# Attention scores with their sign turned: the minimum of the negated scores taken as the bias of the exponentials

## The reference

```python
# first block: 8 heads of 64, causal, with a forget bias
scores = einsum('bqhd,bkhd->bhqk', q_i, k) * scale        # scale = 1/8
scores = scores + c_i[:, :, :, None] - c[:, :, None, :]   # c = cumsum(log_sigmoid(f))
probs = softmax(where(causal, scores, -inf))
out = einsum('bhqk,bkhd->bqhd', probs, v)
# second block, both layers: 4 heads of 64 over 256 memory rows
p = softmax(einsum('bshd,bmhd->bhsm', q, k) * scale); o = p @ v
# second block, second layer: 6 pairs of heads
s = where(allowed, q k^T - slope * |t - pos|, -inf); p = softmax(s)
attn = p[:, :, 0] - lam * p[:, :, 1];  o = attn @ v
```

## Time and profile before

| | us |
|---|---|
| median of three executions | 3593.1 |
| lowest of three executions | 3591.57 |
| the profiled execution | 3596.61 |
| its span in the trace | 3595.3 |
| mean granted TensorE clock over the span | 0.896 |

### The profile page before, as it was taken

The page is one execution under the profiler, slowest core; times in us unless marked ns, Lnnn a source line. Parts: engine busy times, 40 slices in busy tenths (PEclk is TensorE's granted clock), DMA queues, the critical chain, the costliest instruction groups (busy, mean ns, idle before and its releaser), DMA issues.

```text
span 3595.3 us, 49969 instructions
## 1 busy us (share of the span) xinstructions
PE 2998.4 (83%) x20746; PEld 2384.4 (66%) x20746; DVE 1708.5 (48%) x3078; ACT 1071.2 (30%) x1867; POOL 655.5 (18%) x525
## 2 busy tenths in 40 slices
PE   5997857879999999699999677777768899877787
PEld 3775646668888888477886466666556678644466
DVE  2424544454444444665541576775435222466454
ACT  5213454531111111643112122122435111344533
POOL 1112123321111110342110122221014121000013
PEclk8998878989999999899999699998579999888769
DMA  2201003101111111122121000002022112100122
GB/s 71 57 24 59 24 6 117 53 30 53 48 46 54 47 47 47 35 82 71 53 65 63 1 3 3 3 3 90 1 70 70 59 55 68 56 1 1 53 68 73
DMA packets 197458, 164.55 MB, mean 46 GB/s; under 512 B 5312, under 2 KB 173930, under 8 KB 196082
## 3 DMA queue, kind: packets, MB, share of 16 engines
q1 hardware_dynamic: 197234, 161.36, 14.4%
HBM read 138.24 MB, written 23.10 MB: 45 GB/s over the span
## 4 chain that ended last, share of the span: by engine, by line
PE 66%; DVE 15%; ACT 9%; issue 6%; POOL 2%; DMA 2%; DVEq 0%; SPq 0%; ACTq 0%; POOLq 0%
PE ps L659 13%; PE ps L660 13%; PE ps L661 13%; PE ps L1896 5%; PE ps L1597 4%; PE ps L1564 3%; PE ps L1589 2%; ACT sb L1612 2%; PE ps L1302 1%; PE ps L1303 1%; PE ps L1304 1%; DVE r L634 1%; PE ps L700 1%; ACT r L629 1%; PE ps L702 1%
## 5 line engine op out<-in xcount | busy, mean ns | idle before, releaser
L659 PE MATMUL ps<-r,r 128*128 128x512 f32 (+1 forms) x2304 | 930.5, 404 | 131.2 <-DVE r L634 115.3
L660 PE MATMUL ps<-r,r 128*128 128x512 f32 (+1 forms) x2304 | 913.5, 396 | 0.0
L661 PE MATMUL ps<-r,r 128*128 128x512 f32 (+1 forms) x2304 | 911.2, 395 | 0.0
L659 PEld LDWEIGHTS ps<-r,r 128*128 128x128 f32 x2304 | 446.0, 194 | 246.4 <-DVE r L634 115.0
L615 POOL TENSOR_TENSOR sb<-sb 128x1024 f32<-128x1024 f32 x138 | 274.8, 1998 | 1297.4 <-DMA sb<-in_w_ffn_up 491.5
L660 PEld LDWEIGHTS ps<-r,r 128*128 128x128 f32 x2304 | 446.5, 194 | 95.6 <-issue 5.7
L661 PEld LDWEIGHTS ps<-r,r 128*128 128x128 f32 x2304 | 445.8, 193 | 94.2
L1896 PE MATMUL ps<-sb 64*64 64x64 f32 (+2 forms) x8832 | 302.9, 227 | 123.3 <-DVE sb L2146 29.3
L1896 PEld LDWEIGHTS ps<-sb 64*64 64x64 f32 (+1 forms) x8832 | 281.8, 136 | 152.4 <-issue 100.7
L634 DVE TENSOR_TENSOR r<-sb,r 128x1024 fp32r<-128x1024 f32 x198 | 260.4, 1322 | 231.6 <-ACT r L629 231.4
L629 ACT CAST r<-sb 128x1024 fp32r<-128x1024 f32 x198 | 204.9, 1043 | 350.3 <-POOL sb L615 350.1
(11 more groups left out here) (266 smaller groups left out, 3710.7 us busy)
## 6 DMA issues: line engine op xcount, KB each, us to landing
sb<-in_w_out SPq DMA_DIRECT2D x36, 512.0 KB, 4.1
sb<-in_a_w_in SPq DMA_DIRECT2D x29, 512.0 KB, 4.0
sb<-in_w_ffn_gate SPq DMA_DIRECT2D x22, 512.0 KB, 3.9
sb<-in_w_ffn_up SPq DMA_DIRECT2D x22, 512.0 KB, 3.9
sb<-in_w_ffn_down SPq DMA_DIRECT2D x22, 512.0 KB, 3.4
gates<-sb SPq DMA_DIRECT2D x36, 256.0 KB, 2.0
sb<-in_w_in SPq DMA_DIRECT2D x17, 512.0 KB, 4.0
sb<-in_x SPq DMA_DIRECT2D x16, 512.0 KB, 5.6
```

Of the source, the lines that this page charges most:

```text
L659: pe.matmul(self.out, w.hi[:, q, self.cols], hi, start=(q == 0), stop=False)
L660: pe.matmul(self.out, w.hi[:, q, self.cols], lo, start=False, stop=False)
L661: ins = pe.matmul(self.out, w.lo[:, q, self.cols], hi, start=False, stop=(q == w.nk - 1))
```

## The change

q is multiplied by -1/8 in place of 1/8 in all places where it is evicted, so PE delivers negated scores. The biases change their sign too: the scan in `Forget` gives c and not -c, the mask is +1e30, and the distances stay positive. The reduction takes the minimum, which is the negated maximum, and ACT computes exp(-(value) + minimum) by `scale=-1.0`. The 128x1 multiplication by -1 and DVE's wait ahead of it are gone, the event `maxed` with them: ACT waits for `biased`. In `Lambda.dve` the multiplication of the 128x1024 distances by -1 and the wait behind it are gone.

```diff
-            ("negc", [ATT_H, S]), ("xs", [P, KT, S]), ...
+            ("c", [ATT_H, S]), ("xs", [P, KT, S]), ...
...
     def scale_of(self, st):
-        return None if self.silu else 0.125
+        return None if self.silu else -0.125
...
-        dve.tensor_tensor_scan(self.z, self.one, self.a, 0.0, ALU.mult, ALU.subtract).then_inc(*s.step_dve.up("neg_c"))
+        dve.tensor_tensor_scan(self.z, self.one, self.a, 0.0, ALU.mult, ALU.add).then_inc(*s.step_dve.up("c"))
...
-                        act.wait_ge(*s.maxed.at((self.id, i, iq, h)))
+                        act.wait_ge(*s.biased.at((self.id, i, iq, h)))
...
-                        act.activation(self.sc[:, self.buf(iq, h), 0:nk], src, ACT.Exp, bias=s4[:, 1:2],
+                        act.activation(self.sc[:, self.buf(iq, h), 0:nk], src, ACT.Exp, bias=s4[:, 0:1], scale=-1.0,
...
-            dve.tensor_tensor_reduce(self.sc[:, self.buf(iq, h), 0:nk], bank[:, 0:nk], add, 1.0, -3.0e38, ALU.add, ALU.max,
+            dve.tensor_tensor_reduce(self.sc[:, self.buf(iq, h), 0:nk], bank[:, 0:nk], add, 1.0, 3.0e38, ALU.add, ALU.min,
                                      s4[:, 0:1]).then_inc(*s.biased.up((self.id, i, iq, h)))
-            dve.wait_ge(*s.biased.at((self.id, i, iq, h)))
         else:
-            dve.tensor_reduce(s4[:, 0:1], bank[:, 0:nk], AX.X, ALU.max).then_inc(*s.biased.up((self.id, i, iq, h)))
-            dve.wait_ge(*s.biased.at((self.id, i, iq, h)))
-        dve.tensor_scalar(s4[:, 1:2], s4[:, 0:1], -1.0, None, ALU.mult).then_inc(*s.maxed.up((self.id, i, iq, h)))
+            dve.tensor_reduce(s4[:, 0:1], bank[:, 0:nk], AX.X, ALU.min).then_inc(*s.biased.up((self.id, i, iq, h)))
...
-            self.masked = pool.to_reg(NEG)
+            self.masked = pool.to_reg(FAR)
...
         dve.wait_ge(*s.step_act.at("dist"))
-        dve.tensor_scalar(self.dist, self.dist, -1.0, None, ALU.mult).then_inc(*s.step_dve.up("dist"))
-        dve.wait_ge(*s.step_dve.at("dist"))
-        dve.memset(self.dist[0:64, S - 64:S], NEG * 100)
+        dve.memset(self.dist[0:64, S - 64:S], FAR * 100)
...
-    ev_q, ev_k = Evict(k, lambda i: q[:, i, :], 0.125), Evict(k, lambda i: key[:, i, :])
+    ev_q, ev_k = Evict(k, lambda i: q[:, i, :], -0.125), Evict(k, lambda i: key[:, i, :])
```

More of the change, by code:

```diff
@@ L22 @@
 EPS = 1e-6
-NEG = -1.0e30
+FAR = 1.0e30
 HD = 64
@@ L142, in __init__ @@
         self.scratch = {n: nc.dram_tensor(n, shape, F32).ap() for n, shape in (
-            ("negc", [ATT_H, S]), ("xs", [P, KT, S]), ("gates", [P, 10, S]), ("memkv", [2, P, 1024]))}
+            ("c", [ATT_H, S]), ("xs", [P, KT, S]), ("gates", [P, 10, S]), ("memkv", [2, P, 1024]))}
         self.n_ids, self.n_banks = 0, 0
@@ L1068, in dve @@
         dve.wait_ge(*s.step_dve.at("log_f"))
-        dve.tensor_tensor_scan(self.z, self.one, self.a, 0.0, ALU.mult, ALU.subtract).then_inc(*s.step_dve.up("neg_c"))
+        dve.tensor_tensor_scan(self.z, self.one, self.a, 0.0, ALU.mult, ALU.add).then_inc(*s.step_dve.up("c"))
     def sp(self, sp):
         s = self.s
-        sp.wait_ge(*s.step_dve.at("neg_c"))
-        sp.dma_start(self.k.scratch["negc"], self.z).then_inc(*s.dma_misc.up("neg_c", 16))
-        sp.wait_ge(*s.dma_misc.at("neg_c"))
+        sp.wait_ge(*s.step_dve.at("c"))
+        sp.dma_start(self.k.scratch["c"], self.z).then_inc(*s.dma_misc.up("c", 16))
+        sp.wait_ge(*s.dma_misc.at("c"))
 class Pooling(Step):
@@ L1702, in sp_pair @@
             sp.wait_ge(*s.bias_made.at((i - 1, ST - 1, 1)))
-        sp.dma_start(self.cb, self.k.scratch["negc"][2 * i:2 * i + 2, :].partition_broadcast(P)).then_inc(*s.dma_cb.up(("cb", i), 16))
+        sp.dma_start(self.cb, self.k.scratch["c"][2 * i:2 * i + 2, :].partition_broadcast(P)).then_inc(*s.dma_cb.up(("cb", i), 16))
     def pool_scores(self, pool, att, i, iq):
@@ L2770, in layer_b @@
     stores = [EvictStore(k, bufs, k.r, k.rstd_ids, row, True, count) for row in (0, 8)]
-    ev_q, ev_m = EvictNormed(k, lambda i: q[:, i, :], k.r, k.rstd_ids, 0.125), EvictNormed(k, lambda i: q_mem[:, i, :], k.r, k.rstd_ids, 0.125)
+    ev_q, ev_m = EvictNormed(k, lambda i: q[:, i, :], k.r, k.rstd_ids, -0.125), EvictNormed(k, lambda i: q_mem[:, i, :], k.r, k.rstd_ids, -0.125)
     jobs = [(i * P, ev_q, i) for i in range(BT)] + [(2 * BR + i * P, ev_m, i) for i in range(2)]
```

## The result

The changed kernel takes 3597.6 us (median of 15 executions, 3593.4 to 3604.4) against 3591.6 us for the kernel before (median of 15): the ratio is 1.0019, with a 95% interval of 1.0011 to 1.0027. It is slower by some 6 us where 5.4 us less was forecast, and outside the range of 3577 to 3596 us. (One execution of the kernel before, at 7971.73 us, is an outlier; medians don't feel it.)

What follows compares the result with a forecast made beforehand. PE was taken to bound the kernel (83% busy, 66% of the chain), DVE counting only where PE waits for it. Savings of 3.63 + 1.08 + 0.72 = 5.4 us took 3593.1 to 3587.7 us, range 3577 to 3596 us.

Steps and rivals of the forecast that it cites:

- The distances' negation was hidden: The 0.68 us negation of the distances runs in DVE's 1.50 us gaps between evictions, so removing it gains nothing.
- The minimum is no costlier: Minimum takes the maximum's duration; the rival that it costs more, up to 120 us and 3708 us, had chance 0.02.
- PE covers all: Rival: PE's waits are put on DVE only by the trace's order of ends, nothing gained, 3593 us; chance 0.09.
- all 224 count: Rival: every 128x1 negation lies on the path, gain 34.5 us, time 3558.6 us; chance 0.02.
- the 0.72 forecast: Memory attentions: the negation holds the chain once a pair, 4 x 0.18 = 0.72 us saved.
- A term that was too small: Causal attention, 4 pairs: next reduction 0.18 us and copy 0.12 us earlier, 3.63 us saved at blocks and pair starts.
- the sum: Savings in causal, differential and memory attentions: 3.63 + 1.08 + 0.72 = 5.4 us.
- A term too large, of no weight: Differential attention, pair starts: reduction, exponential and scores each about 0.18 us earlier, 6 x 0.18 = 1.08 us saved.
- A PE that idles less has no cause to fall more often: Argument against the clock worsening in the causal attention, where a long low stretch cost about 3.5 us a pair.
- the first rival: Causal attention: more pairs get pair 3's long low-clock stretch, up to 3598.2 us, ends slower; chance 0.11.
- the clock turns against it: Causal attention: the other three pairs become like low-clock pair 3, 3.5 us each, up to 3598.2 us; chance 0.11.
- its own threshold: From two long low-clock stretches on in the causal attention, 7.0 against 5.4 us, the change ends slower.

Runs made afterwards that it cites:

- run 8: Changed kernel plus 21 unread identity products per pair of the differential attention (14, 4 and 3 where PE waits): 3573.7 us, 0.9949 of the kernel before.
- run 12: The kernel before, unaltered, traced and timed once more to see whether its differential stage repeats: 3588.9 us, one execution.
- run 7: Changed kernel with only DVE's wait for its own event kept behind every reduction, the 128x1 operation gone: 3603.3 us, 1.0032 of the kernel before.
- run 9: Kernel before plus 21 unread identity products per pair of the differential attention (14, 4 and 3): 3583.0 us, 0.9977 of the kernel before.
- run 1: Changed kernel, but 128x1 operation (multiplying by 1), its wait and event kept in the differential attention: 3584.0 us, 0.9980 of the kernel before.
- run 2: Changed kernel, but 128x1 operation (multiplying by 1), wait and event gone only in the differential attention, kept elsewhere: 3609.9 us, 1.0052 of the kernel before.
- run 5: Changed kernel, but 128x1 operation, wait and event kept at block 0 of each differential attention pair only: 3579.9 us, 0.9968 of the kernel before.
- run 6: Changed kernel, but 128x1 operation, wait and event kept at blocks 1 to 7 of each differential attention pair: 3587.0 us, 0.9987 of the kernel before.
- run 3: Changed kernel plus 33 unread identity products per pair of the differential attention (20, 7 and 6 where PE waits): 3583.0 us, 0.9975 of the kernel before.
- run 4: Kernel before plus 33 unread identity products per pair of the differential attention (20, 7 and 6): 3592.5 us, 1.0007 of the kernel before.

## Why the prediction was wrong, by its own steps

**What holds.** The 128x1 operation is gone and DVE's busy time is 1670.5 us against the 1673 forecast. The distances' negation was hidden. The minimum is no costlier. The rival "PE covers all" fell, as PE's 4.1 us of waiting for copies went to nothing; "all 224 count" fell with the memory attentions, which gave some 0.9 us for the 0.72 forecast.

**A term that was too small.** I let the next instruction start at the end of the accumulator's reading, 0.18 us earlier for a reduction and 0.12 us for a copy. It starts with the reading, which is the 0.26 us that I had as the upper bound; the copy comes 0.20 us earlier. Pairs of the causal attention with equal clock show it: pair 1 with 13.9 and 13.7 us at 1.2 GHz took 49.9 us before and 48.8 us in the changed kernel, pair 2 with 10.2 us took 48.6 us before and 47.2 us in run 8, so 1.1 and 1.4 us a pair where the sum had 1.04 and 0.91. Run 12 against the changed kernel gives less for pair 2 (17.1 us low in both, 51.3 against 50.4 us) and for pair 3 (6.8 us low in both, 47.5 against 46.4 us): 0.9 and 1.1 us. Over four pairs that is an estimate of some 4.5 us in place of 3.63. The Trainium skill's rule in VectorE: DVE Perf Modes, The DRAIN you can't avoid, that semaphores between chained operations cost nothing extra, would have made the term smaller still; run 7 measured 0.12 us for the wait, so here the measurement decides against it.

**A term too large, of no weight.** In the differential attention I had 0.18 us a pair. Pairs at equal clock: 46.12 and 46.01 us (23.9 us low in both), 39.6 and 39.4 us (none low, runs 9 and 8). So 0.1 to 0.2 us, though the reductions moved by 0.27 us.

**The step that failed.** "A PE that idles less has no cause to fall more often", under the first rival, and with it the sum, which had nothing for the clock. PE does idle less in each pair of the differential attention (10.2 us in pair 2 where it was 10.7, in pair 3 10.2 where it was 13.0), and the stage has 126 us at 1.2 GHz for 65 and is 15.9 us longer. I had priced the clock in the causal attention only (3.5 us a pair, which is about right: the differential attention's 61 us more of low clock cost 15.9 + 1 = 17 us, 0.28 us for each, my figure 0.34) and treated it as noise that either kernel draws from. In the differential attention it isn't noise: runs 1 and 12 repeat the kernel before's pattern and run 2 the changed kernel's, pair by pair. The edit moved the stage from one repeated pattern to another, and pairs 2 to 6, each 2.1 to 3.6 us longer, outweigh every term of the sum. With PE's waits filled (run 8) the changed kernel's stage had 21 us at 1.2 GHz and took 242.3 us, so it is the clock that the 15.9 us went to. The rival "the clock turns against it", at 0.11, is what happened, in another stage than the one in which it was priced; its own threshold, that two long low stretches decide, was passed. A look at the stage's pairs in the kernel before, of which pairs 3 and 5 had 3.4 us at the low level and pairs 1 and 2 had 23.9 and 13.7, would have shown how much hung on the clock there. The prediction also took 2% as the least that the timing tells from no change; the interval of the ratio came out at 0.0008 to either side, some 3 us.

What the rule of the Trainium skill on TensorE's clock (TensorE: Matmul & The Clock Gate, Part 1) says, that the number of matmuls at the lower level varies by phase, agrees with the causal attention's pairs in two executions of one kernel (run 12). It doesn't cover the differential attention, where the phase against the program repeated.

**Open.** Why the rhythm holds against 0.11 us more (run 7) and not against 0.27 us (runs 1, 5, 6) is not settled. That the pairs and the clock's changes pull each other into step is my reading of pairs that all take 44.4 us; no run sets the one and varies the other alone. The kernel before's medians differ by 4.5 us between sittings, which wasn't followed.

## What to carry to other kernels

A small instruction taken off an engine that feeds PE is worth at most its start-to-start distance, wait included, at each place where PE waits for it. But in a stage in which PE waits regularly, look at the granted clock tile by tile in the trace before crediting the sum: a quarter of a microsecond moved a whole stage between two clock patterns, 6% of its length. Filling such waits with harmless products that end about with the wait was worth 25 us against the changed kernel by the ratios (0.9949 and 1.0019), most of it by getting out of the rhythm, and 8 us against the kernel before (run 9); where they lasted too long, 16 us and nothing (runs 3 and 4).

## What the runs showed of the hardware that was not expected

- DVE started the next instruction in the same 10 ns as the reading of the accumulator that belongs to the reduction before it (305.69 and 305.69), when no wait stood between.
- A wait of DVE for its own last event held the next reduction until the one before had ended (354.62, the next at 354.67) and cost 0.12 us of start-to-start distance (0.87 against 0.75 us).
- The differential attention repeated its clock pattern: 65 us at 1.2 GHz in all three traces with the operation in place there (the kernel before twice, run 1), 126 us in all three without it (the changed kernel, runs 2 and 7).
- Both memory attentions ran wholly at 1.2 GHz in every trace (0.50 over 80 us) with PE busy 69.5 of 80 us:

```profile
2527.00:2607.00 80.00, 69.53 (x270) 50.93 (x266) 32.76 (x117) 26.91 (x99) 1.51 (x1) 0.50 0.00 1
```

Nothing here tried to bring that stage to the higher level; the two together are 170 us of the kernel.
